# Reordering the head of a fused two-block transformer kernel, and the steps of the gates among the delta channels

## The reference, cut to what matters

```python
def rms_norm(x, g):
    y = xf * lax.rsqrt(jnp.mean(xf * xf, axis=-1, keepdims=True) + EPS)
    return (y * g)
# first block
h = rms_norm(x, norm_attn[l]);  proj = h @ w_in[l]     # dilated attention's columns are multiplied first
# second block, gated_deltanet
proj = h @ w_in
qkv = silu(causal_depthwise_conv(proj[..., :3 * GDN_WIDTH], conv_w))
a, b = proj[..., 4 * GDN_WIDTH:4 * GDN_WIDTH + 8], proj[..., 4 * GDN_WIDTH + 8:]
beta = sigmoid(b);  g = -exp(a_log) * softplus(a + dt_bias)      # the gates; then a cumulative sum of g
```

## Time and profile before

| | us |
|---|---|
| median of 3 runs | 2692.17 |
| lowest, highest run | 2688.04, 2692.76 |
| the profiled execution's own time | 2689.68 |
| its span | 2688.4 |
| PE busy | 2496.5 (93%) |
| DVE busy | 1227.7 (46%) |
| ACT busy | 864.1 (32%) |
| POOL busy | 439.9 (16%) |

### The profile page before, as it was taken

How to read it: one execution, slowest core, us unless ns; L and a number is a source line. 1 busy time by engine, 2 the same in 40 slices (tenths; PEclk the granted TensorE clock), 3 DMA queues, 4 the chain that set the end, 5 groups by cost and what they waited for, 6 DMA issues and landing times. The chain is left out here.

```text
span 2688.4 us, 37626 instructions
## 1 busy us (share of the span) xinstructions
PE 2496.5 (93%) x15333; PEld 1956.4 (73%) x15333; DVE 1227.7 (46%) x2156; ACT 864.1 (32%) x1572; POOL 439.9 (16%) x467
## 2 busy tenths in 40 slices
PE   7899989899989998999779999999789799999998
PEld 6699987666755554886457888886687777788887
DVE  6876844422321111523445666426556554433333
ACT  3355344422311111333543222224323333322222
POOL 4644704000113332210101000010110200100001
PEclk9899989899989999799889999999899899999999
DMA  5433503023459997331014666323003012232322
GB/s 181 157 113 123 165 19 94 9 83 98 142 215 386 409 408 292 129 94 32 1 55 119 187 189 209 113 78 86 17 3 94 2 33 85 80 98 83 111 83 73
DMA packets 315100, 332.55 MB, mean 124 GB/s; under 512 B 20848, under 2 KB 273904, under 8 KB 302640
## 3 DMA queue, kind: packets, MB, share of 16 engines
q1 hardware_dynamic: 292720, 281.60, 31.9%
q0 software_dynamic: 22208, 48.55, 5.3%
HBM read 372.02 MB, written 16.78 MB: 145 GB/s over the span
## 5 line engine op out<-in xcount | busy, mean ns | idle before, releaser
L350 DVE TENSOR_TENSOR sb_w_lo<-sb_weights,sb_w_hi 128x1024 fp32r<-128x1024 f32 (+2 forms) x221 | 246.8, 1127 | 445.8 <-ACT sb_w_hi L344 445.8
L495 PE MATMUL bank<-sb_h_hi,sb_w_hi 128*128 128x512 f32 x1040 | 422.2, 406 | 8.2 <-DVE sb_w_lo L350 8.2
L497 PE MATMUL bank<-sb_h_hi,sb_w_lo 128*128 128x512 f32 x1040 | 409.1, 393 | 0.0
L496 PE MATMUL bank<-sb_h_lo,sb_w_hi 128*128 128x512 f32 x1040 | 409.0, 393 | 0.0
L344 ACT CAST sb_w_hi<-sb_weights 128x1024 fp32r<-128x1024 f32 x224 | 215.5, 969 | 504.6 <-PE bank L497 438.1
L495 PEld LDWEIGHTS bank<-sb_h_hi,sb_w_hi 128*128 128x128 f32 x1040 | 197.5, 190 | 63.5 <-issue 22.3
L496 PEld LDWEIGHTS bank<-sb_h_lo,sb_w_hi 128*128 128x128 f32 x1040 | 197.6, 190 | 45.7 <-issue 5.3
L497 PEld LDWEIGHTS bank<-sb_h_hi,sb_w_lo 128*128 128x128 f32 x1040 | 197.1, 190 | 43.0
L546 POOL TENSOR_TENSOR sb_scratch<-sb_scratch 128x512 f32<-128x512 f32 x30 | 38.6, 1285 | 1129.9 <-ACT sb_scratch L536 1129.9
L405 PE MATMUL bank<-sb_wide,sb_h_hi 128*128 128x512 f32 (+2 forms) x448 | 178.5, 398 | 11.3 <-DVE sb_wide L387 7.1
L406 PE MATMUL bank<-sb_wide,sb_h_hi 128*128 128x512 f32 (+2 forms) x448 | 172.2, 384 | 0.0
(11 more groups left out here) (561 smaller groups left out, 4549.6 us busy)
## 6 DMA issues: line engine op xcount, KB each, us to landing
sb_weights<-ffn_w_in SPq DMA_DIRECT2D x88, 512.0 KB
sb_weights<-w_in SPq DMA_DIRECT2D x52, 512.0 KB
sb_xT<-ada_w POOLq DMA_DIRECT2D x24, 1024.0 KB, 6.6
sb_weights<-ada_w SPq DMA_DIRECT2D x24, 1024.0 KB
sb_expert_weights<-w_down SPq DMA_DIRECT2D x22, 1024.0 KB
sb_expert_weights<-w_gate SPq DMA_DIRECT2D x20, 1024.0 KB
sb_expert_weights<-w_up SPq DMA_DIRECT2D x19, 1024.0 KB
sb_weights<-ffn_w_out SPq DMA_DIRECT2D x32, 512.0 KB
```

The lines of the kernel that those rows point to most:

```text
L350: dve.tensor_tensor(u.lo[:, 0:u.kt, :], u.chunk.w, u.hi[:, 0:u.kt, :].bitcast(F32), ALU.subtract).then_inc(*k.lo.one())
L495: pe.matmul(bank[:], u.hi[:, kk, :], act[0][:, kk, :], start=first and kk == 0, stop=False)
L496: pe.matmul(bank[:], u.hi[:, kk, :], act[1][:, kk, :], start=False, stop=False)
L497: mm = pe.matmul(bank[:], u.lo[:, kk, :], act[0][:, kk, :], start=False, stop=last and kk == u.kt - 1)
```

## The change

The head's order changes. On SP, the tiles of x go first, then the constants, then the first four weight blocks, and only then distances and router. Each square gets a scratch buffer of its own; DVE adds tiles 0 and 1, 2 and 3, 4 and 5, so that PE sums five tiles and not eight. PE first runs nine products on a buffer of ones that DVE sets, and takes its column of ones from there. The Silu of the condition moves behind the high parts of h. The low part of block 0 moves from POOL to DVE. The waits of engines for the constants move later. In the delta channels only the steps change at which `next(other)` is called: PE 1, 3, 6 become 1, 2, 8; ACT 2, 4, 8 become 1, 3, 9; DVE 3, 5, 7, 9 become 2, 5, 8, 9.

```diff
--- before.py
+++ after.py
@@ -501,27 +501,39 @@
 
 
 
+FOLDED = 3
+
+
 def first_norm(k, gain, arrived, blocks):
 
-    act, pe = k.nc.scalar, k.nc.tensor
+    act, pe, dve = k.nc.scalar, k.nc.tensor, k.nc.vector
     for kk in range(KD):
         act.wait_ge(*arrived[kk])
-        if kk >= 4:
-            act.wait_ge(*k.summed.at(kk - 3))
-        act.activation(k.scr[kk % 4][:], k.xT[:, kk, :], ACT.Square).then_inc(*k.exped.one())
-        pe.wait_ge(*k.exped.at(kk + 1))
+        act.activation(k.scr[kk][:], k.xT[:, kk, :], ACT.Square).then_inc(*k.exped.one())
+    for n in range(FOLDED):
+        dve.wait_ge(*k.exped.at(2 * n + 2))
+        dve.tensor_tensor(k.scr[2 * n][:], k.scr[2 * n][:], k.scr[2 * n + 1][:], ALU.add).then_inc(*k.totalled.one())
+    setup_late_dve(k)
+    pe.wait_ge(*k.padded_dve.at(1))
+    for _ in range(9):
+        pe.matmul(k.bank[0][:, 0:2 * P], k.warm[:, 0:P], k.warm, start=True, stop=True)
+    groups = [2 * n for n in range(FOLDED)] + list(range(2 * FOLDED, KD))
+    for kk in groups:
+        pe.wait_ge(*(k.totalled.at(kk // 2 + 1) if kk < 2 * FOLDED else k.exped.at(kk + 1)))
         for i in range(NT):
-            mm = pe.matmul(k.bank[3][:, i:i + 1], k.scr[kk % 4][:, i * P:(i + 1) * P], k.const("ones")[:, 0:1],
+            mm = pe.matmul(k.bank[3][:, i:i + 1], k.scr[kk][:, i * P:(i + 1) * P], k.warm[:, 0:1],
                            start=kk == 0 and i == 0, stop=kk == KD - 1, skip_group_check=True)
-        mm.then_inc(*k.summed.one())
-    norm_root_act(k, k.summed.at(KD))
+    mm.then_inc(*k.summed.one())
+    pe.wait_ge(k.consts_in, 16)
+    norm_root_act(k, k.summed.at(1))
     block_hi_act(k, blocks[0])
-    block_lo_pool(k, blocks[0])
     block_hi_act(k, blocks[1])
     block_lo_pool(k, blocks[1])
     norm_shift_act(k, None, k.h)
+    setup_act(k)
     norm_inverse_dve(k)
     norm_spread_pe(k)
+    block_lo_dve(k, blocks[0])
     norm_rows_dve(k, gain, None, k.h)
 
 
@@ -1047,10 +1059,14 @@
 
 def setup_sp(k):
     nc, io = k.nc, k.io
-    first = k.at_["dist0"][0]
-    nc.sync.dma_start(k.consts[:], io["consts"][:, 0:first]).then_inc(k.consts_in, 16)
     for kk in range(KD):
         nc.sync.dma_start(k.xT[:, kk, :], io["xT"][kk * P:(kk + 1) * P, :]).then_inc(k.x_in[kk], 16)
+    nc.sync.dma_start(k.consts[:], io["consts"][:, 0:k.at_["dist0"][0]]).then_inc(k.consts_in, 16)
+
+
+def setup_late_sp(k):
+    nc, io = k.nc, k.io
+    first = k.at_["dist0"][0]
     nc.sync.dma_start(k.mixed[:, 0, :], io["consts"][:, first:k.at_["slot"][0]]
                       ).then_inc(k.distances_in, 16)
     nc.sync.dma_start(k.router[:, :, 0:N_GRP], io["w_router_group"].rearrange("(k p) n -> p k n", p=P)
@@ -1071,9 +1087,13 @@
 def setup_dve(k):
     dve = k.nc.vector
     dve.memset(k.eps[:], EPS).then_inc(*k.angled.one())
+    dve.memset(k.warm, 1.0).then_inc(*k.padded_dve.one())
     dve.memset(k.mixed[:, 2:6, :], 0.0)
     dve.memset(k.arena[:, 0:4 * S], 0.0).then_inc(*k.padded_dve.one())
-    dve.wait_ge(k.consts_in, 16)
+
+
+def setup_late_dve(k):
+    dve = k.nc.vector
     dve.wait_ge(k.parameters_in, 48)
     dve.tensor_copy(k.posf[:], k.pos[:]).then_inc(*k.dve_step.one())
     dve.tensor_scalar(k.col["qdil"], k.col["qdil"], HD ** -0.5, None, ALU.mult).then_inc(*k.dve_step.one())
@@ -1082,9 +1102,8 @@
 
 def setup_act(k):
     act = k.nc.scalar
-    act.wait_ge(*k.angled.at(1))
     act.wait_ge(k.parameters_in, 48)
-    act.wait_ge(*k.padded_dve.at(1))
+    act.wait_ge(*k.padded_dve.at(2))
     act.activation(k.cond[:], k.col["c"], ACT.Silu).then_inc(*k.act_step.one())
     k.cond_ready = k.act_step.last()
 
@@ -1095,6 +1114,7 @@
     k.pos = k.sb("pos", [P, 2 * NT], I32)
     k.roots = k.sb("roots", [P, NT])
     k.eps, k.kgain, k.early = k.sb("eps", [P, 1]), k.sb("kgain", [P, 1]), k.sb("early", [P, 1])
+    k.warm = k.scr[12][:, 0:2 * P]
     k.posf = k.sb("posf", [P, 2 * NT])
     k.cos1, k.sin1 = k.sb("cos1", [P, NT, ROPE // 2]), k.sb("sin1", [P, NT, ROPE // 2])
     k.cos2, k.sin2 = k.sb("cos2", [P, NT, ROPE2 // 2]), k.sb("sin2", [P, NT, ROPE2 // 2])
@@ -1116,8 +1136,7 @@
     setup_sp(k)
     setup_pool(k)
     setup_dve(k)
-    setup_act(k)
-    k.nc.tensor.wait_ge(k.consts_in, 16)
+    k.nc.scalar.wait_ge(*k.angled.at(1))
 
 
 
@@ -1259,7 +1278,7 @@
     for p, after_next in zip(all_pieces, all_pieces[2:] + [None, None]):
         p.later = after_next
     other = angles_dve(k)
-    k.nc.vector.wait_ge(k.distances_in, 16)
+    k.nc.vector.wait_ge(k.consts_in, 16)
     for g in range(GROUPS):
         blocks = plans[g]
         pieces = all_pieces[8 * g:8 * g + 8]
@@ -1271,7 +1290,9 @@
             for _ in other:
                 pass
             angles_act(k)
-        load_weights_sp(k, [b.chunk for b in blocks])
+        load_weights_sp(k, [b.chunk for b in blocks[0 if g else 4:]])
+        if g == 0:
+            k.nc.vector.wait_ge(k.distances_in, 16)
         modulation_pool(k, pieces)
         k.meet()
 
@@ -2991,7 +3012,7 @@
                 split_pair_pe(k, units[0], units[1], h, k.bank[0:2])
             elif s > 1 or hg > 0:
                 split_product_pe(k, units[s], h, k.bank[s % 4])
-        if s in (1, 3, 6):
+        if s in (1, 2, 8):
             next(other, None)
         n = s - 3
         if 0 <= n < NCH:
@@ -3040,7 +3061,7 @@
                 act.activation(acc[:], k.heads[part][:, hh, :], ACT.Square).then_inc(*k.squared.one())
         for u in units[s + 4:s + 5]:
             split_hi_act(k, u)
-        if s in (2, 4, 8):
+        if s in (1, 3, 9):
             next(other, None)
         n = s - 4
         if HG <= n < NCH:
@@ -3070,7 +3091,7 @@
                                      op0=ALU.mult, op1=ALU.add).then_inc(*done.one())
         for u in units[n + 4:n + 5]:
             split_lo_dve(k, u)
-        if n in (3, 5, 7, 9):
+        if n in (2, 5, 8, 9):
             next(other, None)
         if n == 5:
             query_rows_dve(k, hg)
@@ -3640,6 +3661,8 @@
         query = [b for half in range(2)
                  for b in plan_blocks(k, w_in, C_MLAQ + half * 4 * MLA_D, 4 * MLA_D, first=4 * half)]
         latent = plan_blocks(k, w_in, C_CKV, KV_RANK + ROPE, first=8)
+        load_weights_sp(k, [b.chunk for b in plans[0][:4]])
+        setup_late_sp(k)
         first_norm(k, lambda kk: columns(k.col["norm_attn"], kk), [(sem, 16) for sem in k.x_in], plans[0])
         dilated(k, plans, query)
         back = mla(k, query, latent)
```

## The result

The changed kernel takes 2673.32 us as the median of 4 runs (2670.48 to 2678.28), beside 2691.19 for the kernel before: a ratio of 0.9937, with a 95% interval of 0.9925 to 0.9949. The experiments timed it again: 2675.18, ratio 0.9950 (0.9936 to 0.9963). It is faster, and the forecast of 2675.0 lies within the runs of both. The profiled execution took 2670.48, 19.2 us less than that of before; it is the fastest of its four.

What follows compares the result with a forecast made beforehand. PE is busy for 93% of the span, so gains come only from its waits and slow clock. Head 10.6 plus gates 6.0 made 16.6 us off 2689.68: 2673.1, given as a median of 2675, range 2668 to 2684.

Steps and rivals of the forecast that it cites:

- Head: Start of the kernel: first row of h 10.2 us earlier plus 0.4 from low parts, 10.6 us, bounds 7.5 and 12.
- the end of the sums: Head: PE's one-column sums end at 15.6 us, first two groups fast, last three at half clock; bounds 12.7 and 17.9.
- the two chains behind it: Head: block 0's low part ends at 16.8, block 1's high part at 16.9, both before the first row at 18.3.
- Low parts: Head: POOL's low part of block 1 no longer holds DVE, 1.8 us less; after the Silu's 1.5, 0.4 gained.
- The rule of a drain: Head, moved Silu: about 1.38 us extra per table change would give 1.4 us less; the prediction went by the trace instead.
- Rival 1: Head: transfers land out of issue order, or sums stay at half clock; head 8 us or less, 2678 to 2684; chance 0.14.
- Gates: Delta channels: waits and clock losses fall from 9.6 to 3.6 us, a gain of 6.0, bounds 4.4 and 7.7.
- The step laid out by hand: Delta channels: PE still waits 2.0 us for ACT's copy before the transposes; the wait before the cumulative products goes.
- the clock loss behind the wait: Delta channels: 1.65 us lost to half clock after the remaining wait before the transposes, between nothing and 3.0.
- Rival 2: Delta channels: the first wait costs what it did; gates gain 3 to 4.5 us, total about 14, 2678; chance 0.13.
- The copy's cover for ACT's last part: Delta channels, step 9: ACT's loads delay the transposes' copy by 1.9 us, but PE asks later; cost zero, up to 1.9.
- Rival 3: Between 50 and 120 us: new holds between DVE and POOL eat the gain, nothing measurable or slower; chance 0.05.

Runs made afterwards that it cites:

- e2: Kernel before the change, with only the new steps of the gates in the delta channels: 2683.98 us, ratio 0.9980 to before.
- e3: Changed kernel with the gates' old steps put back, so the head's change alone: 2681.81 us, ratio 0.9968 to before.
- e1: The changed kernel unedited, timed again: 2675.18 us, ratio 0.9950 to the kernel before.
- e12: Changed kernel with a fourth pair added on DVE and the Silu between squares and root: 2673.41 us, ratio 0.9938 to before.
- e4: Changed kernel with PE's transposes of the gates at step 3 instead of 2: 2675.15 us, ratio 0.9952 to before.
- e11: Changed kernel with PE's transposes at step 3 and ACT's last gates part behind the copy of step 9: 2676.65 us, ratio 0.9945 to before.
- e10: Changed kernel with a fourth pair added on DVE and five products on ones behind the first group: 2672.81 us, ratio 0.9936 to before.
- e5: Changed kernel without the nine products on ones: 2673.95 us, ratio 0.9941 to before.

## Why the prediction was right, and where its terms were off

The sum was 16.6 us off 2689.68; the profiled execution gained 19.2, the medians 17.9 and 14.7. Sign, range and mechanism held: both halves gain, and by e2 and e3 independently. That the sum came so near is in part luck: the head gave 2 us or more less than predicted and the gates 1.5 us more.

**Head: 10.6 predicted, 8.6 measured at the first row, 8.2 at the attention.** The term that was mis-sized is the end of the sums: 15.6 taken, 17.10 measured, within the bounds of 12.7 and 17.9. Of the 1.5 us, 0.6 is x (last square 11.65 taken, 12.21 measured), and 0.9 is one more group at half clock: four were slow and not three. "The first two groups fast" was a guess of when the clock falls. In the change PE's wait behind the first group, 1.21 us, was followed by half clock at once; in e1, the same code, the wait was 2.29 us and the second group fast, as guessed, but x was later (last square 13.08), and the sums ended at 16.96. In the five traces with this head the first row comes 7.3 to 8.7 us ahead of 28.49; the lower bound that the prediction gave was 7.5. What makes the clock fall there no run shows. The transfers were told well: x landed at 11.6 (11 predicted), the constants at 13.8 (13.3), block 0 at 15.2 (14.6). The step from the sums to the first row was taken as 2.74 and was 19.93 - 17.10 = 2.83, so the two chains behind it were told rightly: the spreading is released by DVE's reciprocal, not by the constants.

**Low parts.** I had POOL's low part of block 1 end at 19.3, ahead of the first row's low part. It ended at 21.81, since both high parts stand behind the root in ACT's queue, which my step had bounded by the landing alone, and the sums were late as well. DVE's first L637 took 1.01 us and not 0.7 (2.48 before): 1.5 of the 1.8 us came. Block 2's product starts 33.98 - 19.93 = 14.05 us behind the first row, within the 13.6 to 14.3 given and on the side that I did not take. No gain came from there: the 0.4 is gone.

**The table load.** The rule of a drain of some 1.38 us (the Trainium skill, ScalarE: Activation LUTs, What ACT_TABLE_LOAD costs) does not show at the moved Silu: the load starts at 30.00, the high part before it ends at 29.98, and the Silu starts 1.30 us after the load. By e12, two changes of table and the Silu between 13.29 and 16.10 cost 2.8 us, which is 1.28 + 0.21 + 1.28.

**Rival 1** half came. The sums ran at half clock nearly throughout, as it said in its last sentence, and the head gained 8.6 in the profiled execution, and 7.3 to 7.6 in e3, e4 and e11, where it said 8 or less. Its own mechanism did not come for what the head waits for: x, constants and weights landed in the order of their issue (x by 13.4, block 0 at 16.3, block 1 at 17.7 in e10, where ACT waits for each). The Trainium skill (DMA: Bandwidth & Descriptors, Queues, rings and completion order) says that completion need not be in order. The traces agree, for transfers that nobody waits for here: in e10 SP issues the distances at 9.15 and the router's first transfer at 11.53, and by the last column, us from issue to landing, the first lands at 9.15 + 11.9 = 21.05 and the second at 11.53 + 8.2 = 19.73.

```profile
sb_mixed<-consts SPq DMA_DIRECT2D x1, 256.0 KB, 11.9
sb_router<-w_router_group SPq DMA_DIRECT2D x1, 16.0 KB, 8.2
```

So the order of issue held here and is not a thing to build on.

**Gates: 6.0 predicted, 7.5 measured.** The step laid out by hand was right to 0.04 us: the wait before the transposes is 1.96 (2.0 predicted), the one before the cumulative products is gone. The mis-sized term is the clock loss behind the wait, 1.65 taken, nothing measured: the clock is 1.00 behind it in each of the ten traces that have this wait (1.93 to 2.00 us). The prediction had taken it by the nearest length, 2.04 us. Rival 2 (the wait costs what it did) did not come: without that loss the sum is 9.6 - 2.0 = 7.6, and the trace gives 7.5. The copy's cover for ACT's last part held, at 0.

**Rival 3** did not come. From the first row to the attention's first exponential it is 97.1 us before and 97.5 after: both engines moved together, and no hold was added.

**What the profiled execution has beyond that**, 19.2 - 8.2 - 7.5 = 3.5 us, is not the change's as far as the traces show: e1, the same code, has the root of the second norm at 1094.28, where the trace of the change has 1090.81. Before it was at 1100.98 (1100.94 in e2). By e1, e3 and e4 the head is worth 6.7 to 6.9 us at that place, and with the 7.5 of the gates that is 14.2 to 14.4, near the 14.7 of the medians; where between 117 and 1094 us the executions part stays open. So 2673.1 for that execution erred by two errors, 2.4 us too much at the head and 1.5 too little in the gates, and by that drift.

## What to carry to other kernels

When a stretch is one chain of waits, look first for the unrelated instruction that an in-order queue holds ahead of it: the Silu, of 1.5 us of work, held all squares until its parameters had landed and was worth 3.2 to 4.7 us at the sums. A wait between generators is best placed by laying out each engine's step with measured durations, and moving it until nobody is asked early, but its clock loss is not told by its length (2.0 us cost nothing more, 1.37 us some 1.35 more); if the loop behind it is bound by other engines (6.54 us a step here), removing the rest of the wait only moves it. Work that shortens something beside a transfer, as the products on ones did, gains nothing until the transfer is no longer later.

## What the runs showed of the hardware that I had not expected

- One-column sums keep or lose the clock in ways that PE's busy time does not tell. In the change 32 run at 0.215 us each, PE busy without a gap, at a granted clock of 0.50; in e10, with ten wide products ahead, the next 16 run at 0.131, after waits of 1.50 and 0.28 us; in e12 and in e1 eight run at full clock (1.05 us) after waits of 3.03 and 2.29 us, and those behind them at 0.224 and 0.185; in e4, after a wait of 3.10 us, 32 run at 0.218. What decides was not found. In the kernel before, 64 take 0.215 each although the clock column reads 1.00 there, so durations have to be looked at beside that column.
- A wait of 1.93 to 2.00 us before the transposes was followed by full clock in all ten traces that have it (the change, e1, e2, e5 to e10, e12). The waits of 2.04 and 2.06 us before the cumulative products, in the kernel before and in e3, were followed by a lower one (0.50 for 3.3 us; 0.69 from 1871 to 1875). Length alone does not decide: the wait of 1.37 us in e4 and e11 was followed by 0.50 for 2.7 us. Ahead of that one stand 8 one-column products, ahead of the others 24 wide ones. Whether that is the reason was not tried.
- The first product of block 0 took 0.99 us in the change, at a granted clock of 0.50 (19 to 22 us), and 0.47 in e5, without the products on ones; from first row to first product it is 1.96 and 1.54 us. The fills are not shown to be the cause: e3 and e11, which have them, took 0.59 and 0.58.
- The squares' table load waits for the first tile of x (3.46, released by it), while the root's load runs at 12.23, ahead of ACT's wait for the sums (root at 17.14). So a load need not stand behind the wait of the instruction that it serves, and the first one's 1.28 us might lie beside the transfer; that was not tried. It would gain nothing in the change and in e1, where ACT waits for x again behind the first two squares (1.83 and 3.14 us).
